# The first block's layers written out, the ends of its layers handed on tile by tile, and the last modulation sum between two tiles

## The chip, the cores and the metric

The kernel runs on one core of a Trainium2 chip. The metric is the device time of one execution in microseconds (us). The engines are PE (TensorE, matrix products), DVE (VectorE), ACT (ScalarE), POOL (GpSimd) and SP (SyncE); SP and POOL issue transfers here. Each engine runs its own instructions in the order in which they are written, and waits for the others on semaphores.

## The reference

x has 256 rows (tokens) of 1024 float32 numbers. A first block of two layers (projections, two kinds of attention, gates, an output projection, a layer norm) is followed by a second block of two layers, whose sublayers are modulated: a shift, a scale and a gate per sublayer come from a conditioning vector c by a product with mod_w.

```python
def first_block(x, w_in, ..., w_out, ln_gamma, ln_beta):
    for l in range(DEPTH):                       # 2
        h = x @ w_in[l]
        ...                                      # MLA and differential attention, gates
        out = merged @ w_out[l]
        x = _layer_norm(DEEPNORM_ALPHA * x + out, ln_gamma[l], ln_beta[l])
    return x

def half_ffn_sublayer(x, mod, j, wi, wo, g, b):
    y = 0.5 * swiglu(modulate(x, mod, j), wi, wo)
    return post_norm_update(x, y, mod, j, g, b)

def second_block(x, c, ctx, c_ctx, mod_w, mod_b, ...):
    for i in range(DEPTH):
        mod_lat = (silu_c @ mod_w[i] + mod_b[i]).reshape(-1, N_MOD, D_MODEL)
        x = half_ffn_sublayer(x, mod_lat, 0, ...)
        mod_ctx = (silu_cc @ mod_w[i] + mod_b[i]).reshape(1, N_MOD, D_MODEL)   # layer 0
        ctx_s = half_ffn_sublayer(ctx_s, mod_ctx, 0, ...)
        ...                                      # window attention (0) or fourier mix (1)
        x = half_ffn_sublayer(x, mod_lat, 2, ...)
```

## The kernel before

The 256 tokens are two tiles of 128 rows, tile 0 and tile 1 (t in the code). Float32 products are made from three matmuls of rounded halves: w_hi by xT_hi, w_lo by xT_hi, w_hi by xT_lo, one after the other (L558, L559, L560), added in one bank (acc0 to acc3). A full projection of 512 columns is 8 such triples for each tile, 48 matmuls for both. The left operand of a product must have its features on the partitions, so x is turned first: PE transposes 128x128 blocks into the banks turn0, turn1, score0 and score1 (L577, or L595 tile by tile), ACT copies them rounded into xT_hi (L1115 plain, L1126 or L1308 with scale and shift of the modulation), and DVE makes xT_lo, the rest (L1490 plain, L1501 and L1502 modulated).

Weights come in pieces of two times 512 columns. SP loads them into raw; ACT rounds one to w_hi (L1087) once PE has freed its place, DVE makes w_lo (L1455). There are 4 places (SPLIT_SLOTS), and the splits run 3 pieces (LEAD) ahead of the projection. A piece is free when tile 1 has used it.

The first block is a loop over LAYERS = 2, in hardware (c.loop) on SP, POOL, PE, ACT and DVE. A wait on a semaphore compares with a register there that grows with the turn of the loop, and REGISTER_ALU instructions compute it; behind the loop the counts are constants. The first projection of a layer is 416 columns wide (LOW). In the loop it is made by project, which takes x turned whole and goes piece by piece, both tiles for each piece. The last projection of a layer, w_out, makes output columns 0 to 511 first (acc0, acc1) and then columns 512 to 1023 by project_by_tile (acc2 for tile 0, acc3 for tile 1): tile 0 with all four pieces, then tile 1 with the same four. first_done is raised behind tile 0.

Behind w_out stands the layer norm. For each tile DVE adds the product to x (L1801), takes the mean (L1544), multiplies (L1549), waits for ACT's square sum and root (L1151, L1153), and writes x (L1555), which raises x_ready. ACT has two splits ahead of its first square sum, and these wait for pieces that tile 1 frees.

Behind some sublayers of the second block (attention, fourier, FFN) the next projection already starts tile by tile: project_first turns tile 0, makes its products with 2 pieces, turns tile 1 and makes the rest. Inside the first block it doesn't.

The modulation vectors of the second block's first layer are made in passing by the first block. POOL loads mod_w chunk by chunk into mod_raw. DVE multiplies a chunk's 8 features by the conditioning and adds them up, for the context and for the latent (L1575, two instructions a feature, the last one into mod_sum_lat); PE sums over the partitions with 4 one-column matmuls for each of the two (mod_sum, L670), and DVE stores the result with the bias (mod_store, L1592, L1593). At a layer's end two chunks are summed: one sum stands between the two halves of w_out's projection, the last one behind it. The features 6 and 7 of the last chunk stand on DVE behind the two additions of acc0 and acc1 and ahead of the norm.

## Time and profile before

| | us |
|---|---|
| median of 3 runs | 1699.57 |
| lowest and highest | 1698.55, 1700.25 |
| the profiled execution, its own time | 1696.36 |
| its span, first to last instruction | 1694.6 |
| PE busy | 1601.3 |
| DVE busy | 1207.7 |
| ACT busy | 802.3 |
| mean granted clock of PE | 0.971 |

The rows further down are from the profiled execution. Their times run from the start of its span. A matmul's length in a row overlaps the next one's start, so that the distance of two starts is what one costs in a row of them. A granted clock of 1.00 is 2.4 GHz, 0.50 is 1.2 GHz.

### The profile page before, as it was taken

What the parts mean: (1) busy time and instruction counts of PE and PEld (TensorE: products, weight loads), DVE (VectorE), ACT (ScalarE), POOL (GpSimd) and SP (SyncE); (2) the same over time, 40 slices, a digit from 0 to 9 for tenths busy, and PEclk for the clock granted to TensorE, in tenths of its full rate; (3) what the DMA queues carried; (4) which work ended last, traced back from release to release, by engine and by line L of the source; (5) the groups of instructions that cost most, each with busy time, mean ns of one, the idle gap of its engine ahead of it and who ended that gap; (6) DMA issues with size and microseconds to landing.
All of it is one profiled execution on the core that took longest, in us unless ns stands there. A gap on an engine that the chain in (4) does not pass through costs nothing.

```text
span 1694.6 us, 23800 instructions
## 1 busy us (share of the span) xinstructions
PE 1601.3 (94%) x7635; PEld 1311.9 (77%) x7635; DVE 1207.7 (71%) x1849; ACT 802.3 (47%) x1242; POOL 140.1 (8%) x205
## 2 busy tenths in 40 slices
PE   6989989989889999999999798999999999989997
PEld 5877778877678878888788457887888878878876
DVE  6877888877887775677757766777487765475545
ACT  5565535455444444444534465444354443254442
POOL 1100001100011110011100011111001110000000
PEclk9999988999989999999999899999999999999999
DMA  8763448743568888588858105988768885466551
GB/s 313 270 208 128 150 152 310 249 169 112 175 219 267 275 270 233 163 280 275 228 181 243 50 1 173 308 275 270 206 212 275 276 232 176 124 177 196 184 183 55
DMA packets 200497, 349.41 MB, mean 206 GB/s; under 512 B 11188, under 2 KB 128236, under 8 KB 199900
## 3 DMA queue, kind: packets, MB, share of 16 engines
q1 hardware_dynamic: 174668, 252.90, 47.2%
q0 software_dynamic: 25744, 95.43, 17.6%
q8 instruction: 47, 0.77, 0.2%
q14 instruction: 38, 0.31, 0.1%
HBM read 347.21 MB, written 1.08 MB: 206 GB/s over the span
## 4 chain that ended last, share of the span: by engine, by line
PE 86%; DVE 8%; issue 3%; ACT 2%; DMA 0%; SPq 0%; DVEq 0%; ACTq 0%
PE acc L558 25%; PE acc L560 25%; PE acc L559 25%; DVE w_lo L1455 2%; PE score L682 2%; PE turn L886 1%; PE acc L794 1%; PE score L973 1%; PE score L670 1%; PE score L774 1%; DVE att_work L2007 1%; PE turn L783 1%; PE score L838 1%; DVE wide L1783 0%; PE score L577 0%
## 5 line engine op out<-in xcount | busy, mean ns | idle before, releaser
L1455 DVE TENSOR_TENSOR w_lo<-raw,w_hi 128x1024 fp32r<-128x1024 f32 (+1 forms) x490 | 586.0, 1200 | 294.3 <-ACT w_hi L1087 287.7
L1087 ACT ACTIVATE w_hi<-raw 128x1024 fp32r<-128x1024 f32 (+1 forms) x490 | 508.2, 1042 | 563.8 <-PE acc L560 561.4
L558 PE MATMUL acc<-w_hi,xT_hi 128*128 128x512 f32 (+1 forms) x1456 | 586.8, 403 | 23.1 <-DVE xT_lo L1502 8.5
L560 PE MATMUL acc<-w_hi,xT_lo 128*128 128x512 f32 (+1 forms) x1456 | 574.6, 395 | 0.0
L559 PE MATMUL acc<-w_lo,xT_hi 128*128 128x512 f32 (+1 forms) x1456 | 574.1, 394 | 0.0
L558 PEld LDWEIGHTS acc<-w_hi,xT_hi 128*128 128x128 f32 x1456 | 279.4, 192 | 83.1 <-issue 25.7
L560 PEld LDWEIGHTS acc<-w_hi,xT_lo 128*128 128x128 f32 x1456 | 278.6, 191 | 59.2
L559 PEld LDWEIGHTS acc<-w_lo,xT_hi 128*128 128x128 f32 x1456 | 279.6, 192 | 54.6
L458 POOL DMA_DIRECT2D mod_raw<-in_mod_w x144 | 104.0, 723 | 963.5 <-DVE mod_run L1575 777.4
L558 PE MATMUL acc<-w_hi,hT_hi 128*128 128x512 f32 x440 | 174.3, 396 | 0.8 <-DVE hT_lo L1916 0.8
L560 PE MATMUL acc<-w_hi,hT_lo 128*128 128x512 f32 x440 | 173.6, 395 | 0.0
L559 PE MATMUL acc<-w_lo,hT_hi 128*128 128x512 f32 x440 | 173.6, 395 | 0.0
L1575 DVE SCALAR_TENSOR_TENSOR mod_run<-mod_raw,silu_c,mod_run 128x512 f32<-128x512 f32 x216 | 161.1, 746 | 4.3 <-DMA mod_raw<-in_mod_w 4.2
L558 PEld LDWEIGHTS acc<-w_hi,hT_hi 128*128 128x128 f32 x440 | 82.8, 188 | 21.1 <-DVE hT_lo L1916 2.0
L560 PEld LDWEIGHTS acc<-w_hi,hT_lo 128*128 128x128 f32 x440 | 82.8, 188 | 19.6
L559 PEld LDWEIGHTS acc<-w_lo,hT_hi 128*128 128x128 f32 x440 | 82.8, 188 | 19.2
L1319 ACT ACTIVATE silu_g<-acc 128x256 f32<-128x256 f32 x110 | 36.2, 381 | 86.8 <-PE acc L560 86.8
L1909 DVE TENSOR_TENSOR hidden<-acc,silu_g 128x256 f32<-128x256 f32 x110 | 41.5, 419 | 16.1 <-ACT silu_g L1319 16.1
L1575 DVE SCALAR_TENSOR_TENSOR acc_ctx<-mod_raw,silu_c,acc_ctx 128x512 f32<-128x512 f32 x70 | 52.2, 746 | 0.0
L1916 DVE TENSOR_TENSOR hT_lo<-turn,hT_hi 128x512 f32 (+1 forms) x55 | 38.0, 692 | 9.7 <-ACT hT_hi L1323 3.5
L1228 ACT ACTIVATE work<-score,neg_max 128x256 f32<-128x256 f32 x64 | 29.7, 473 | 28.8 <-DVE neg_max L1685 28.8
L886 PE MATMUL turn<-ident,hidden 128*128 128x128 f32 x220 | 33.1, 273 | 4.4 <-DVE hidden L1909 4.4
(259 smaller groups left out, 1266.0 us busy)
## 6 DMA issues: line engine op xcount, KB each, us to landing
raw<-in_ffn_wi SPq DMA_DIRECT2D x220, 512.0 KB, 5.0
mod_raw<-in_mod_w POOLq DMA_DIRECT2D x144, 512.0 KB, 4.4
raw<-in_ffn_wo SPq DMA_DIRECT2D x110, 512.0 KB, 4.8
raw<-in_w_in SPq DMA_DIRECT2D x72, 512.0 KB, 5.2
raw<-in_w_out SPq DMA_DIRECT2D x16, 512.0 KB, 4.5
raw<-in_attn_wqkv SPq DMA_DIRECT2D x16, 512.0 KB, 4.6
wide<-in_b_merge POOLq DMA_DIRECT2D x4, 1024.0 KB, 8.3
raw<-in_w_branch_a SPq DMA_DIRECT2D x8, 512.0 KB, 4.2
```

Source lines behind the costliest of these rows:

```text
L458: pool.dma_start(mod_raw[:, s, :, :], w_mod[l, :, 2 * i:2 * i + 2, at]).then_inc(mod_in[s], 16)
L558: nc.tensor.matmul(dst, xh, wh, start=start, stop=False)
L559: nc.tensor.matmul(dst, xh, wl, start=False, stop=False)
L560: return nc.tensor.matmul(dst, xl, wh, start=False, stop=stop)
L682: m = nc.tensor.matmul(bank["score1"][:, 4 * i + j:4 * i + j + 1], mod_kept[:, i, j * P:j * P + P], ones[:, 0:1], start=True, stop=True)
L886: m = nc.tensor.transpose(dst[:, f * TOK + t * P:f * TOK + t * P + P], hidden[:, half, t, f * P:f * P + P], ident[:])
L1087: nc.scalar.activation(w_hi[:, i % SPLIT_SLOTS, 0:n], raw[:, s, i % 2 * PIECE:i % 2 * PIECE + n], ACT.Copy).then_inc(hi_ready, 1)
L1319: nc.scalar.activation(silu_g[:, half, t, :], bank[ACC[2 * half + t]][:, FC:2 * FC], ACT.Silu).then_inc(silu_done, 1)
L1455: nc.vector.tensor_tensor(w_lo[:, i % SPLIT_SLOTS, 0:n], raw[:, i // 2 % RAW_SLOTS, i % 2 * PIECE:i % 2 * PIECE + n], w_hi[:, i % SPLIT_SL ...
L1575: m = nc.vector.scalar_tensor_tensor(out=end if k == KD - 1 else run, in0=w, scalar=by, in1=run, op0=ALU.mult, op1=ALU.add)
L1909: nc.vector.tensor_tensor(hidden[:, half, t, :], bank[b][:, 0:FC], silu_g[:, half, t, :], ALU.mult).then_inc(moved[b], 1)
L1916: nc.vector.tensor_tensor(sl(hT_lo), bank[b][:], sl(hT_hi).bitcast(F32), ALU.subtract).then_inc(moved[b], 1)
```

## The change

1. The loops over the layers of the first block are written out (`for l in range(LAYERS)`) on all five engines, so that counts are constants. piece_width knows the widths of the second layer's pieces too.
2. Each layer's first projection is made by project_first, given the width 416. The norm ahead of it (in ACT's norm_root and DVE's layer_norm) contains the copies of tile 0: plain_tile(0) behind the first layer, turn_tile(0) with the modulation behind the second. Four pieces are split ahead of it, not 3. The start of the kernel, where x comes from memory, has the same order. The second block's first FFN starts by tile too (early=1).
3. PE's last modulation sum of a layer moves from behind project_by_tile to between its tiles. DVE's mod_store of it, with mods_stored, moves from behind the norm to between the addition of acc2 and the mean of tile 0.

```diff
 def piece_width(i):
-    i = i % LAYER_PIECES if i < LAYER_PIECES + LEAD else 0
+    i = i % LAYER_PIECES if i < LAYERS * LAYER_PIECES else 0
...
-            def project_first(banks, kept):
+            def project_first(banks, kept, n=512):
...
-            def project_by_tile(banks):
+            def project_by_tile(banks, between=None):
...
                     if t == 0:
                         m.then_inc(first_done, 1)
+                        if between:
+                            between()
...
-            with c.loop(pe, LAYERS, per):
-                after = turn(lambda t, k: x[:, t, k * P:k * P + P], x_tile)
+            for l in range(LAYERS):
...
-                project(ACC[0:2], 4, n=LOW, after=after)
+                project_first(ACC[0:2], False, LOW)
...
                 project(ACC[0:2], 4, after=after)
                 mod_sum(True)
-                project_by_tile(ACC[2:4])
-                mod_sum(True)
+                project_by_tile(ACC[2:4], lambda: mod_sum(True))
...
-            after = ffn(turn_x(), True, turn_ctx_in, by_tile=False)
+            after = ffn(None, True, turn_ctx_in, by_tile=False)
...
+            def plain_tile(t):
+
+                for half in range(2):
+                    src = filled(turn_bank(2 * t + half))
+                    nc.scalar.activation(xT_hi[:, 4 * half:4 * half + 4, t * P:t * P + P], src[:].rearrange("p (k n) -> p k n", k=4),
+                                         ACT.Copy).then_inc(turn_hi, 1)
+
             split(LEAD)
-            with c.loop(act, LAYERS, per):
-                turn_plain(xT_hi)
+            plain_tile(0)
+            split()
+            for l in range(LAYERS):
+                plain_tile(1)
...
-                norm_root()
+                norm_root(x, SPLIT_SLOTS, (lambda: plain_tile(0)) if l < LAYERS - 1 else (lambda: turn_tile(mod_lat[:, 0, :], 0, 0)))
...
-            nc.scalar.preload_act_table(ACT.Silu)
-            turn_modulated(mod_lat[:, 0, :], 0)
-            ffn(x, True, (mod_ctx, 0))
+            second_tile(0, 0)
+            ffn(x, True, (mod_ctx, 0), early=1)
...
                     add(t, 1)
+                    if t == 0:
+                        mod_store(*ctx_chunk(4))
+                        mods_stored()
...
-                layer_norm(update, lambda t: wide[:, t, 0:D], between=split)
-                mod_store(*ctx_chunk(4))
-                mods_stored()
+                layer_norm(update, lambda t: wide[:, t, 0:D], between=split, at_root=split,
+                           before_end=(lambda: plain_tile(0)) if l < LAYERS - 1 else (lambda: turn_tile(0)))
```

How the instructions stand on the engines, before and after. In these rows the line, the operation, what it writes and reads, its size and the semaphores it waits for are given; the lines of after are those of the changed file.

PE before, the switch from tile 0 (acc2) to tile 1 (acc3) in the last projection of the first layer:

```order
L558 MATMUL acc2<-w_hi,xT_hi 128x512
L559 MATMUL acc2<-w_lo,xT_hi 128x512
L560 MATMUL acc2<-w_hi,xT_lo 128x512
L558 MATMUL acc3<-w_hi,xT_hi 128x512
L559 MATMUL acc3<-w_lo,xT_hi 128x512
L560 MATMUL acc3<-w_hi,xT_lo 128x512
```

PE after, the same place:

```order
L560 MATMUL acc2<-w_hi,xT_lo 128x512
L672 MATMUL score1<-ones,mod_sum_lat 128x1 [waits score1_moved,mod_step]
L672 MATMUL score1<-ones,mod_sum_lat 128x1 x3
L672 MATMUL score1<-ones,acc_ctx 128x1 x4
L558 MATMUL acc3<-w_hi,xT_hi 128x512
L559 MATMUL acc3<-w_lo,xT_hi 128x512
L560 MATMUL acc3<-w_hi,xT_lo 128x512
```

The sum's matmuls (score1) now stand between, with the wait for mod_step, which DVE raises behind each feature.

PE before, behind the last product of that projection, to x's first transposes:

```order
L560 MATMUL acc3<-w_hi,xT_lo 128x512
L666 REGISTER_ALU
L541 REGISTER_ALU [waits mod_step]
L670 MATMUL score1<-ones,mod_sum_lat 128x1 [waits score1_moved]
L670 MATMUL score1<-ones,mod_sum_lat 128x1 x3
L670 MATMUL score1<-ones,acc_ctx 128x1 x4
L112 REGISTER_ALU
L112 COMPARE_AND_BRANCH
L577 MATMUL turn0<-ident,x 128x128 [waits turn0_moved,x_ready]
L577 MATMUL turn0<-ident,x 128x128
L577 MATMUL turn1<-ident,x 128x128 [waits turn1_moved]
```

PE after, the same place:

```order
L560 MATMUL acc3<-w_hi,xT_lo 128x512
L595 MATMUL turn0<-ident,x 128x128 [waits turn0_moved,x_ready]
L595 MATMUL turn0<-ident,x 128x128 x3
L595 MATMUL turn1<-ident,x 128x128 [waits turn1_moved]
L595 MATMUL turn1<-ident,x 128x128 x3
L558 MATMUL acc0<-w_hi,xT_hi 128x416 [waits turn0_moved,lo_ready,acc0_moved]
L559 MATMUL acc0<-w_lo,xT_hi 128x416
L560 MATMUL acc0<-w_hi,xT_lo 128x416
```

The sum and the loop's end are gone; 8 blocks of tile 0 are turned, and its products with 416 columns follow at once.

DVE before, from feature 7 of the last chunk to the next layer:

```order
L1575 SCALAR_TENSOR_TENSOR acc_ctx<-mod_raw,silu_c,acc_ctx 128x512 [waits ctx_step]
L1571 REGISTER_ALU
L1575 SCALAR_TENSOR_TENSOR mod_sum_lat<-mod_raw,silu_c,mod_run 128x512 [waits mod_step]
L1801 SCALAR_TENSOR_TENSOR x,x_sum<-x,acc2 128x512 [waits first_done,ln_in]
L1811 REGISTER_ALU
L1544 SCALAR_TENSOR_TENSOR neg_mean<-x_sum,mean_factor 128x1 [waits acc2_moved]
L1548 REGISTER_ALU
L1549 SCALAR_TENSOR_TENSOR wide<-x,neg_mean,ln_rows 128x1024 [waits mean_ready]
L1554 RECIPROCAL inv_std<-inv_std 128x1 [waits std_ready]
L1461 REGISTER_ALU
L1555 SCALAR_TENSOR_TENSOR x<-wide,inv_std,ln_rows 128x1024 [waits dve_step]
L1453 REGISTER_ALU
```

and behind the norm of tile 1:

```order
L1555 SCALAR_TENSOR_TENSOR x<-wide,inv_std,ln_rows 128x1024 [waits dve_step]
L1464 REGISTER_ALU
L1592 ISA [waits score1_full]
L1592 TENSOR_TENSOR mod_ctx<-score1,modb 128x4
L1593 REGISTER_ALU
L1593 TENSOR_TENSOR mod_lat<-score1,modb 128x4
L1596 MEMSET free 128x1
```

DVE after, the same stretch up to the first copies of the turned tile:

```order
L1598 SCALAR_TENSOR_TENSOR acc_ctx<-mod_raw,silu_c,acc_ctx 128x512 [waits ctx_step]
L1598 SCALAR_TENSOR_TENSOR mod_sum_lat<-mod_raw,silu_c,mod_run 128x512 [waits mod_step]
L1824 SCALAR_TENSOR_TENSOR x,x_sum<-x,acc2 128x512 [waits first_done,ln_in]
L1615 TENSOR_TENSOR mod_ctx<-score1,modb 128x4 [waits score1_full]
L1616 TENSOR_TENSOR mod_lat<-score1,modb 128x4
L1619 MEMSET free 128x1
L1567 SCALAR_TENSOR_TENSOR neg_mean<-x_sum,mean_factor 128x1 [waits acc2_moved]
L1572 SCALAR_TENSOR_TENSOR wide<-x,neg_mean,ln_rows 128x1024 [waits mean_ready]
L1577 RECIPROCAL inv_std<-inv_std 128x1 [waits std_ready]
L1578 SCALAR_TENSOR_TENSOR x<-wide,inv_std,ln_rows 128x1024 [waits dve_step]
L1458 TENSOR_TENSOR w_lo<-raw,w_hi 128x1024 [waits hi_ready]
L1824 SCALAR_TENSOR_TENSOR x,x_sum<-x,acc3 128x512 [waits piece_done]
```

The store of the sum stands between the addition of acc2 and tile 0's neg_mean, and waits there for score1_full.

ACT before, the entry of the loop at the start:

```order
L1087 ACTIVATE w_hi<-raw 128x1024 [waits piece_done,raw_in1]
L112 UNCONDITIONAL_BRANCH
L112 ISA
L1115 ACT_TABLE_LOAD
L1115 ACTIVATE xT_hi<-turn0 128x512 [waits turn0_full]
L1115 ACTIVATE xT_hi<-turn1 128x512 [waits turn1_full]
```

ACT after, the same place:

```order
L1085 ACTIVATE w_hi<-raw 128x1024 [waits piece_done,raw_in0]
L1085 ACTIVATE w_hi<-raw 128x1024 [waits piece_done]
L1085 ACTIVATE w_hi<-raw 128x1024 [waits piece_done,raw_in1]
L1173 ACTIVATE xT_hi<-turn0 128x4x128 [waits turn0_full]
L1173 ACTIVATE xT_hi<-turn1 128x4x128 [waits turn1_full]
```

The loop's entry and its table load are not there.

## Rows read from the trace of the kernel before

**Rows 1.** The page, busy time and share of the engines
```profile
PE 1601.3 (94%) x7635; PEld 1311.9 (77%) x7635; DVE 1207.7 (71%) x1849; ACT 802.3 (47%) x1242; POOL 140.1 (8%) x205
```

**Rows 2.** Timeline of PE, first layer's end: start, us, engine, line, out<-in, idle
```profile
234.67 0.95 PE L670 MATMUL score<-ones,mod_sum_lat 128*128 128x1 f32 x8
236.37 0.48 PE L558 MATMUL acc<-w_hi,xT_hi 128*128 128x512 f32 x1
...
241.94 0.39 PE L558 MATMUL acc<-w_hi,xT_hi 128*128 128x512 f32 x1
```

**Rows 3.** Timeline of DVE, the same stretch
```profile
236.67 0.16 DVE L1592 TENSOR_TENSOR mod_ctx<-score,modb 128x4 f32 x1 [0.89 <-PE score L670]
...
243.89 0.75 DVE L1575 SCALAR_TENSOR_TENSOR mod_sum_lat<-mod_raw,silu_c,mod_run 128x512 f32<-128x512 f32 x1
```

**Rows 4.** Timeline of PE behind tile 1
```profile
247.39 0.95 PE L670 MATMUL score<-ones,mod_sum_lat 128*128 128x1 f32 x8
...
251.02 1.11 PE L577 MATMUL turn<-ident,x 128*128 128x128 f32 x4 [1.79 <-issue]
...
254.20 0.69 PE L577 MATMUL score<-ident,x 128*128 128x128 f32 x2 [1.64 <-DVE mod_lat L1593]
...
257.70 0.71 PE L558 MATMUL acc<-w_hi,xT_hi 128*128 128x416 f32 x1 [1.10 <-DVE xT_lo L1490]
```

**Rows 5.** Timeline of ACT, the same stretch
```profile
254.95 1.28 ACT L1115 ACT_TABLE_LOAD   x1 [2.46 <-issue]
```

**Rows 6.** Windows: us, busy and count of each engine, PEclk, DMA share, GB/s
```profile
257.70:263.40 5.70, 5.70 (x16) 5.44 (x17) 5.70 (x12) 2.61 (x4) 0.00 (x0) 0.50 0.80 277
263.40:269.45 6.05, 6.05 (x33) 6.00 (x32) 6.05 (x8) 2.12 (x2) 0.72 (x1) 1.00 0.80 235
241.94:269.45 27.51, 22.97 (x105) 20.85 (x104) 23.67 (x42) 13.50 (x18) 2.16 (x3) 0.75 0.45 143
478.68:507.80 29.12, 23.39 (x106) 19.40 (x105) 22.49 (x36) 15.21 (x22) 3.25 (x5) 0.82 0.60 209
```

**Rows 7.** Timeline of PE and ACT behind the second block's attention
```profile
1036.91 0.39 PE L560 MATMUL acc<-w_hi,xT_lo 128*128 128x512 f32 x1
...
1039.47 2.91 ACT L1308 ACTIVATE turned_more<-turn,mod_lat 128x128 f32<-128x128 f32 x8 [0.44 <-PE turn L595]
...
1042.59 0.77 PE L558 MATMUL acc<-w_hi,xT_hi 128*128 128x512 f32 x1 [2.79 <-DVE xT_lo L1502]
...
1048.43 1.11 PE L595 MATMUL score<-ident,x 128*128 128x128 f32 x8 [0.38 <-DVE x L1555]
1049.29 0.47 PE L558 MATMUL acc<-w_hi,xT_hi 128*128 128x512 f32 x1
```

**Rows 8.** Timeline of DVE, second layer's end
```profile
480.63 0.75 DVE L1575 SCALAR_TENSOR_TENSOR mod_sum_lat<-mod_raw,silu_c,mod_run 128x512 f32<-128x512 f32 x1
```

**Rows 9.** Timeline of PE and a window, two shorter idle stretches
```profile
169.24 0.49 PE L558 MATMUL acc<-w_hi,xT_hi 128*128 128x512 f32 x1 [1.49 <-DVE wide L1708]
...
457.90 1.93 PE L577 MATMUL score<-ident,wide 128*128 128x128 f32 x8 [3.37 <-DVE wide L1788]
...
461.34 0.44 PE L559 MATMUL acc<-w_lo,xT_hi 128*128 128x512 f32 x1
...
169.20:172.60 3.40, 3.37 (x15) 2.81 (x16) 3.33 (x8) 3.30 (x11) 0.00 (x0) 1.00 0.30 83
```

**Rows 10.** Chain of 30 to 241 by line, one piece; DVE's timeline beside it
```profile
by line: PE acc L558 21.0%; PE acc L560 20.0%; PE acc L559 20.0%; issue 7.0%; PE acc L794 4.6%; DVE w_lo L1455 3.7%; PE score L670 3.2%; PE score L774 3.1%; PE turn L783 2.4%; PE score L838 2.0%; DVE wide L1783 2.0%; DVE acc_ctx L1575 1.2%;
...
201.90 0.50 issue
...
201.74 0.75 DVE L1575 SCALAR_TENSOR_TENSOR acc_ctx<-mod_raw,silu_c,acc_ctx 128x512 f32<-128x512 f32 x1
202.40 0.75 DVE L1575 SCALAR_TENSOR_TENSOR mod_run<-mod_raw,silu_c,mod_run 128x512 f32<-128x512 f32 x1
```

**Rows 11.** Timeline of ACT at the start
```profile
15.69 1.28 ACT L1115 ACT_TABLE_LOAD   x1
```

More of the change, by code:

```diff
@@ L698, in _ @@
             m.then_inc(full[b], 1)
[L700 to L703 removed]
+            for l in range(LAYERS):
                 def turn_latents():
@@ L1493, in turn_plain, with plain_tile @@
                         split_after(g)
+            def plain_tile(t):
+                for half in range(2):
+                    b = turn_bank(2 * t + half)
+                    c.next(b)
+                    dve.wait_ge(turn_hi, c.next("hi"))
+                    sl = lambda r: r[:, 4 * half:4 * half + 4, t * P:t * P + P]
+                    nc.vector.tensor_tensor(sl(xT_lo), bank[b][:].rearrange("p (k n) -> p k n", k=4), sl(xT_hi).bitcast(F32),
+                                            ALU.subtract).then_inc(moved[b], 1)
+                    if t == 0 and half == 0:
+                        split()
             def turn_scaled_group(g, hi, lo, place):
@@ L1605, in _ @@
             split()
-            per = {"split": 64, "piece": 64, "step": 50, "mod": 48, "mod_ctx": 40, "mod_in0": 12, "mod_in1": 12, "turn0": 16, "turn1": 16, "score0": 11, "score1": 17, "acc0": 6, "acc1": 6,
-                   "hi": 10, "low_sq": 1, "low_std": 1, "acc1 moved": 14, "acc3 moved": 12, "bias": 32, "gates": 1,
-                   "diff_sq": DHEADS, "diff_std": 1, "mean": NT, "std": NT, "scaled": 4, "acc2 moved": 12, "ln": 32, "first": 1, "rotated": 1}
-            with c.loop(dve, LAYERS, per) as l:
-                turn_plain(xT_hi, xT_lo, splits=True)
+            plain_tile(0)
+            split()
+            for l in range(LAYERS):
+                split()
+                plain_tile(1)
                 for i, src in enumerate((cols[:, bass.ds(2 * l + G_Q, 1)], cols[:, bass.ds(2 * l + G_Q + 1, 1)],
```

56 lines of the change are left out of this document (25 added, 31 removed).

## The prediction, made before the changed kernel ran

> **What bounds the kernel now.** I read the page's totals first: PE is busy 94% of 1694.6 us [rows 1], the next engine 71%. So the time moves only where PE stands still, runs at the lower of its two clocks, or gets work. The list of PE's idle stretches then says where the change can matter: the end of each layer of the first block. There I read PE's timeline, then DVE's and ACT's beside it, then the windows.
>
> First layer's end. Tile 0 of w_out's projection is over and tile 1 starts at 241.94 [rows 2]. PE ends tile 1, makes the last modulation sum at 247.39, turns x in two bursts with idle of 1.79 and 1.64 us, and starts the next layer's products at 257.70 [rows 4]. The second burst is released by DVE's mod_lat, which stands right behind x of tile 1. ACT loads its table at 254.95, with the turned x waiting [rows 5]. The first 16 products (128x416) then take 5.70 us at a granted clock of 0.50 (1.2 GHz), the 33 behind them 6.05 us at 1.00 (2.4 GHz) [rows 6]. The projection behind that starts at 269.45. From 241.94 that is 27.51 us; the second layer's end, from 478.68 to the FFN's second projection at 507.75, takes 29.1 [rows 6].
>
> The same hand-over by tile as the change makes already runs behind the attention of the second block. Last product 1036.91, so the next slot would be 1037.14; ACT scales the turned tile 0 from 1039.47; products again at 1042.59, 12 of them; tile 1 is turned at 1048.43; products again at 1049.29 [rows 7]. That is 5.45 us to the restart and 5.84 us more to tile 1's turn.
>
> **The change, part by part.**
>
> *1. The last modulation sum between tile 0 and tile 1.* Its 16 one-column matmuls cost 1.70 us (234.67 to 236.37) wherever they stand [rows 2]. But they read what DVE makes of features 6 and 7, and DVE starts the last of these at 243.89 and ends it at 244.64 [rows 3], while PE is through with tile 0 at 241.94. Today that costs nothing, as tile 1 is between. Now PE waits 2.70 us. Queued behind the wait are tile 1's 24 products and all after them. Can DVE come sooner? It waits for the layer's first sum (idle 0.89, released by PE's score at 236.67 [rows 3]) and is busy without a break from there to 244.64: 7.9 us of work against 24 products of PE, 5.57 us. Both are tied to the same instant and the change puts nothing else in between, so the wait is 2.7, with 0.3 of doubt. The second layer's last feature starts at 480.63 and ends at 481.38 [rows 8], tile 0 at 478.68: 2.70 again.
>
> *2. What that wait does to the clock.* No row shows an idle of 2.7 us in a full-speed stretch. The nearest from below: 1.49 us ahead of 169.24, and the window that starts with it stays at 1.00 [rows 9]: nothing lost. From above: 3.37 us ahead of 457.90, after which PE is at half clock until the shorter product of 461.34 [rows 9], 3.4 us of which half is lost, 1.7; the cold stretch of 257.70 to 263.40 would make it 2.85. Idle with 1.7 us of one-column matmuls behind it makes 4.4 us in which PE streams almost nothing, so I lean to the upper row and take 2.0, with 0 to 2.9 as bounds. The Trainium skill, TensorE: Matmul & The Clock Gate, section HAM oscillation, says that a wait between bursts which is long enough makes the next burst start at the low clock, every time over; by it the end would pay twice, here and at the hand-over; it also means that a shorter one is free, and then the sum would be 2.0 less at each end.
>
> *3. Hand-over by tile, first end.* PE ends tile 1 at 241.94 + 2.70 + 1.70 + 5.45 + 2.0 = 253.8 (5.45: window of 241.94 to 247.39, the rows' difference). The restart comes 5.45 later in the row behind the attention. Here ACT makes 2 plain copies for its 8 scaled ones of 2.91 us [rows 7], and DVE drops the cast and the gate's multiply. DVE's other work between stays, so not all of that is won; I estimate 1.0 less, so 4.4: 258.2. Tile 1 is turned 5.8 later, 264.0, as DVE and ACT do the same norm between. The 12 narrow products ahead of it hide in that. Turning takes 0.86 at full clock (1048.43 to 1049.29), 1.7 at half; 1.3, since 4.2 us of cold products with idle behind are less than the 5.70 that it took today. The 36 products left take 36 x 0.19 = 6.8, plus 0.5 for those still cold. Next projection: 264.0 + 1.3 + 6.8 + 0.5 = 272.6, against 269.45: **+3.1**.
>
> Without the wait and its cold stretch (4.7) it would be 267.9, 1.6 better than now: the hand-over by tile is worth that, and the moved sum costs more.
>
> *4. Second end.* The same to 478.68 + 11.85 = 490.5. Restart 5.2 later (scaled copies stay; only the gate's multiply is gone), 495.7; to the products of tile 1's second part 6.7 as behind the attention; then 36 products of 128x512 at 0.2275, 8.2: 510.6 against 507.75: **+2.8**.
>
> *5. The start.* The table load of 1.28 us at the loop's entry [rows 11] is not there in the changed order, and PE waits for what stands behind it. Given back: tile 1 is now turned between products (0.9 to 1.7), where it was hidden before. -0.4 to +0.4 by that alone; tile 1's products also need a fourth piece split earlier, on DVE, and PE can start after half the work: -1.3 at best, +0.5 at worst, I take **-0.5**.
>
> *6. The loops written out.* Register arithmetic, the jump back and the ACT table load at the loop's head go. The jump's 1.79 us of PE idle (released by "issue", 251.02 [rows 4]) ended before x of tile 1 was there, so it hid behind DVE. I take 0; from 0 to what the third rival says. Register work ahead of DVE's instructions leaves no gap: at 201.74 two follow one another 0.66 apart, with no idle listed between [rows 10]. DVE's store of the sum now stands ahead of tile 0's norm and waits for PE until 246.4. Behind the store are neg_mean and one product of x, done by about 248.5; what x of tile 0 then waits for is ACT's root, which stands behind two splits that need the first two pieces freed by tile 1 (246.3 + 2.9, a split and the squares: past 251). So the store is hidden by over 2 us; without that cover each us of it would be a us. Loads on SP's and POOL's queues keep their order; transfers are not what PE waits for here.
>
> Sum: 3.1 + 2.8 - 0.5 = **+5.4 us**. The profiled run took 1696.36 with a span of 1694.6; it would be 1701.8 now. The median of the runs shown is 1699.57, 3.2 above the profiled run, so I forecast 1699.57 + 5.4 = **1705.0**. A measurement of this kernel can tell about 0.2%, 3.4 us, from no change.
>
> **Rivals.**
>
> *A. The forecast*, wait and cold stretch at both ends: 1703 to 1707.
>
> *B. The wait is there but the clock holds*, as behind the 1.49 us idle. Each end 2.0 better, +1.4 in all, 1701.0; with half of it lost, +3.4. For it: 2.7 is nearer to 1.49 than to 3.37. Against it: the matmuls of one column behind it. It gives "the same". The rule of the Trainium skill named above has room for both.
>
> *C. The other side: the loops cost more than their gaps show.* The chain of waits of 30 to 241 gives "issue" 7.0%, 14.8 us of a layer, 29.6 in two [rows 10]; pieces of it are 0.50 us long inside DVE's work. Were that register arithmetic, writing out would take a third of it away: -10, with the +5.4 of the rest the time is 1695.0. It decides from 5.4 us, a fifth of this share; under it the kernel isn't faster. Against it: DVE's rows lie end to end there, so the "issue" is time of an instruction that overlaps its neighbour's.
>
> *D. It gets worse.* If PE is at half clock also for the 12 products, tile 1's turn and the whole of the rest, because the two gaps leave too little between them, each end loses 2 more (the 36 narrow products at 0.35 for 12 of them): +9.4, 1709.
>
> **How the numbers follow.** A 0.52, B 0.26, C 0.12, D 0.10. B lies inside 0.2%, C is faster, A and D slower: 0.12, 0.26, 0.62. The range takes all of A and B (down to +0.5 for a gain of 1.3 at the start, 1700.1), most of D, up to 1709.0, and the near part of C, down to 1697.5, where writing out would be worth 7.5.
>
> **What will show it.** Right: in each layer's end an idle of 2.7 us ahead of the sum's first matmul, released by DVE's mod_sum_lat; 24 products of tile 1 of which the first ones stand 0.427 apart; the restart 4.4 (5.2) behind the last; tile 1's turn 5.8 later; no table load at the start. The stretch from tile 0's end to the next projection is 30.6 and 31.9 us. B: products 0.2275 apart right behind the sum. C: the middle of each layer, from 30 to 230, is shorter by more than 2 us with the same PE work. Wrong altogether would be an end with no idle at the sum, since all rests on DVE being as late as it is now.

## The result, and the profile after

The changed kernel takes 1716.91 us (median of 4 runs, 1716.32 to 1719.07); the kernel before took 1699.06 beside it. The ratio is 1.0112, with a 95% interval of 1.0097 to 1.0127: about 18 us slower, where 5.4 were forecast. The forecast had the sign and missed the range, which ended at 1709.0. The profiled execution has a span of 1715.2 us, 20.6 more than before; the medians are 17.9 apart, since the profiled execution of before (1696.36) was 2.7 us under its median and this one (1716.99) lies on it.

To find where they come from, one takes the same piece of work in both traces and subtracts its starts. The stages are cut at products that can be told by their shape: the first product of 512 columns of a layer (its second projection), the first of 384 columns, the switch from tile 0 to tile 1 in w_out.

| Stretch | before | after | longer by | forecast |
|---|---|---|---|---|
| span's start to the first layer's second projection | 30.34 | 29.02 | -1.3 | -0.5 |
| first layer: second projection to the 384-column products | 60.2 | 67.5 | +7.3 | 0 |
| from there to the switch of tiles | 151.4 | 149.4 | -2.0 | 0 |
| first end: switch to the next layer's second projection | 27.5 | 30.5 | +3.0 | +3.1 |
| second layer: second projection to the 384-column products | 60.2 | 66.8 | +6.6 | 0 |
| from there to the switch of tiles | 149.0 | 149.9 | +0.8 | 0 |
| second end: switch to the FFN's second projection | 29.1 | 33.3 | +4.2 | +2.8 |
| everything behind it | | | +2.0 | 0 |
| sum | | | +20.6 | +5.4 |

So the three places that the forecast looked at came out within 1.4 us of it, and two thirds of the loss lie where it said nothing: at the beginning of each layer, some 20 us behind the hand-over.

The page of the changed kernel, busy time and the chain by engine. Against [rows 1], PE has 6 us more of busy time for the same 7635 instructions (products at half clock), DVE's work is the same, and 2% of the chain that ended last is now DMA, where it was 0%:

```profile
PE 1607.4 (94%) x7635; PEld 1314.3 (77%) x7635; DVE 1206.8 (70%) x1849; ACT 801.6 (47%) x1248; POOL 140.5 (8%) x205
...
PE 81%; DVE 13%; ACT 3%; DMA 2%; issue 2%; SPq 0%; DVEq 0%; ACTq 0%
```

**The beginning of a layer.** PE's timeline behind the first layer's second projection (start, us, engine, line, out<-in, count, and in brackets the idle time ahead and who ended it):

```profile
49.88 0.50 PE L558 MATMUL acc<-w_hi,xT_hi 128*128 128x512 f32 x1 [1.61 <-DVE w_lo L1458]
...
57.57 0.76 PE L558 MATMUL acc<-w_hi,xT_hi 128*128 128x512 f32 x1 [2.95 <-DVE w_lo L1458]
```

PE waits for a split of weights twice, 1.61 and 2.95 us, and is at half clock behind the second wait: eleven products from 57.57 on, 0.63 us long instead of 0.39 and 0.43 apart instead of 0.23, which is some 2.3 us more. The three together are 6.9 of the 7.3 us. Neither wait is there before. DVE's timeline says what it did instead of splitting:

```profile
26.98 1.23 DVE L1458 TENSOR_TENSOR w_lo<-raw,w_hi 128x1024 fp32r<-128x1024 f32 x1 [2.83 <-ACT w_hi L1085]
28.12 0.48 DVE L1596 TENSOR_SCALAR acc_ctx<-mod_raw,silu_c 128x512 f32<-128x512 f32 x1
...
48.60 1.22 DVE L1458 TENSOR_TENSOR w_lo<-raw,w_hi 128x1024 fp32r<-128x1024 f32 x1
55.41 0.49 DVE L1596 TENSOR_SCALAR acc_ctx<-mod_raw,silu_c 128x512 f32<-128x512 f32 x1 [5.58 <-DMA mod_raw<-in_mod_w]
...
56.20 1.22 DVE L1458 TENSOR_TENSOR w_lo<-raw,w_hi 128x1024 fp32r<-128x1024 f32 x1
```

Read the brackets. At 26.98 DVE waited for ACT's w_hi of the fifth piece. The first two features stand behind that split, so they come at 28.12; before, at 23.66, though PE's products started 1.5 us later then. Then at 55.41 DVE waits 5.58 us for a DMA: the second chunk of mod_w. The split at 56.20 is queued behind it, and that is the one that PE wants at 57.57.

Why was the fifth piece late? ACT, the same time:

```profile
16.44 1.05 ACT L1085 ACTIVATE w_hi<-raw 128x1024 fp32r<-128x1024 f32 x1
21.99 1.09 ACT L1173 ACTIVATE xT_hi<-score 128x512 fp32r<-128x512 f32 x2 [4.50 <-PE score L595]
25.89 3.32 ACT L1085 ACTIVATE w_hi<-raw 128x1024 fp32r<-128x1024 f32 x3 [2.81 <-PE acc L560]
```

ACT waits 2.81 us for a product of PE to free a place. A piece is free when tile 1 has used it. In the projection piece by piece that is after 12 products; tile by tile it is after 30, with the turning of tile 1 among them: 24 of tile 0 and 6 of tile 1.

Why was the chunk late? POOL's timeline of the changed kernel, from the third load of the first chunk to the first load of the second chunk:

```profile
31.76 0.72 POOL L458 DMA_DIRECT2D mod_raw<-in_mod_w  x1 [21.36 <-DVE mod_run L1598]
36.68 0.72 POOL L458 DMA_DIRECT2D mod_raw<-in_mod_w  x1 [4.20 <-DVE mod_run L1598]
37.40 1.11 POOL L485 DMA_DIRECT2D wide<-in_b_merge  x2
38.50 0.53 POOL L466 DMA_DIRECT2D ln_rows<-in_ln_gamma  x1
39.02 0.53 POOL L467 DMA_DIRECT2D ln_rows<-in_ln_beta  x1
41.60 0.72 POOL L458 DMA_DIRECT2D mod_raw<-in_mod_w  x1 [2.04 <-DVE mod_run L1598]
```

and of the kernel before:

```profile
27.64 0.72 POOL L458 DMA_DIRECT2D mod_raw<-in_mod_w  x1 [16.49 <-DVE mod_run L1575]
...
33.49 1.11 POOL L485 DMA_DIRECT2D wide<-in_b_merge  x2
...
38.11 0.72 POOL L458 DMA_DIRECT2D mod_raw<-in_mod_w  x1 [2.47 <-DVE mod_run L1575]
```

POOL issues in order, and its third load waits for DVE's first two features: 31.76 against 27.64. Behind it in the queue stand another mod load, the merge bias (2 x 1 MB) and the norm's rows (2 x 0.5 MB), and only then the second chunk: 41.60 against 38.11. That is 3.5 us later; but the load landed 13.8 us after its issue (55.4), where before it took 11.6 (49.7). Windows of the changed kernel (us, busy and count of PE, PEld, DVE, ACT, POOL, then PEclk, DMA share, GB/s):

```profile
26.00:34.00 8.00, 8.00 (x39) 7.11 (x39) 7.02 (x10) 6.01 (x7) 0.72 (x1) 1.00 0.33 105
42.00:56.00 14.00, 11.01 (x56) 8.98 (x54) 7.24 (x23) 8.06 (x17) 1.05 (x2) 0.99 1.02 399
```

From 26 to 34 the transfers run at a third of their time with nothing to fetch, and from 42 to 56 the transfers come at 399 GB/s, with the 3 MB among them. (Before, they are as dense from 40 to 50 us, at 398 GB/s, but the chunk's load was issued earlier.) The chunk lands 5.7 us later than before: 3.5 by its issue and 2.2 by its longer way.

**The ends of the layers.** PE at the first end, from tile 0's last product to the second projection's neighbour; it answers to [rows 2] and [rows 4]:

```profile
245.69 0.39 PE L560 MATMUL acc<-w_hi,xT_lo 128*128 128x512 f32 x1
248.45 1.05 PE L672 MATMUL score<-ones,mod_sum_lat 128*128 128x1 f32 x8 [2.37 <-DVE mod_sum_lat L1598]
...
250.34 0.77 PE L558 MATMUL acc<-w_hi,xT_hi 128*128 128x512 f32 x1
...
258.97 1.10 PE L595 MATMUL turn<-ident,x 128*128 128x128 f32 x8 [1.41 <-DVE x L1578]
...
261.66 0.68 PE L558 MATMUL acc<-w_hi,xT_hi 128*128 128x416 f32 x1 [1.59 <-DVE xT_lo L1505]
...
268.64 0.70 PE L558 MATMUL acc<-w_hi,xT_hi 128*128 128x416 f32 x1
```

The idle ahead of the sum is there and released by DVE's mod_sum_lat: 2.37 us (2.7 were forecast from where PE's next product would start; counted so, 245.91 to 248.45, it is 2.54). The products start at half clock (0.77), the restart is 4.3 behind tile 1's last slot (forecast 4.4), tile 1's products another 7.0 on. The second end:

```profile
495.65 1.64 PE L672 MATMUL score<-ones,mod_sum_lat 128*128 128x1 f32 x8 [2.38 <-DVE mod_sum_lat L1598]
497.15 1.84 PE L672 MATMUL score<-ones,acc_ctx 128*128 128x1 f32 x8
498.86 0.77 PE L558 MATMUL acc<-w_hi,xT_hi 128*128 128x512 f32 x1
...
511.40 0.77 PE L558 MATMUL acc<-w_hi,xT_hi 128*128 128x512 f32 x1 [2.50 <-DVE xT_lo L1517]
```

Here the sum itself ran at half clock, 1.64 and 1.84 us where it takes 0.95 and 1.03 [rows 4], 3.2 from start to start instead of 1.7. That is 1.5 us which the forecast did not have, and it missed 1.4 at this end. From its first product to the slot behind its last, tile 1 takes 7.1 us at the first end (250.34 to 257.40) and 7.4 at the second, for 5.45 of work. Windows of it, each to the end of its last product, granted clock 0.78 and 0.74:

```profile
250.34:257.56 7.22, 7.22 (x25) 5.52 (x25) 1.78 (x6) 3.71 (x6) 0.00 (x0) 0.78 0.00 0
498.86:506.42 7.56, 7.56 (x25) 5.74 (x25) 1.81 (x6) 3.73 (x6) 0.00 (x0) 0.74 0.00 0
```

### The profile page after: what moved, and what is told of

It reads as the page before. It is cut to its first block, busy times and chain, and to the rows that moved or that the text cites. A ratio compares the mean times of both kernels' runs of the same rounds, so it can differ in the third digit from the quotient of the medians.

```text
span 1715.2 us, 22567 instructions
## 1 busy us (share of the span) xinstructions
PE 1607.4 (94%) x7635; PEld 1314.3 (77%) x7635; DVE 1206.8 (70%) x1849; ACT 801.6 (47%) x1248; POOL 140.5 (8%) x205
## 4 chain that ended last, share of the span: by engine, by line
PE 81%; DVE 13%; ACT 3%; DMA 2%; issue 2%; SPq 0%; DVEq 0%; ACTq 0%
PE acc L558 24%; PE acc L560 23%; PE acc L559 23%; DVE w_lo L1458 4%; DMA mod_raw<-in_mod_w 2%; PE score L684 1%; PE turn L884 1%; PE acc L793 1%; DVE x L1578 1%; PE score L672 1%; PE score L971 1%; DVE acc_ctx L1598 1%; PE score L773 1%; DVE att_work L2024 1%; ACT w_hi L1085 1%
## 5 line engine op out<-in xcount | busy, mean ns | idle before, releaser
L558 PEld LDWEIGHTS acc<-w_hi,xT_hi 128*128 128x128 f32 x1456 | 281.0, 193 | 94.7 <-issue 30.5
```

The source lines that it names most:

```text
L558: nc.tensor.matmul(dst, xh, wh, start=start, stop=False)
```

## The experiments

Times are medians, each beside runs of the kernel before on the same chip; a ratio is to that kernel, with its 95% interval. "Changed kernel" is the one that was predicted. The kernel before took 1699.06 us beside the changed kernel, 1698.55 beside experiments 1 to 4, 1700.12 beside 5 to 7 and 1701.29 beside 8 to 10, so a difference of two medians from different groups is uncertain by 2 to 3 us.

### 1. Only the loops written out

```diff
-            with c.loop(dve, LAYERS, per) as l:
+            for l in range(LAYERS):
```

(the same on the other four engines, in the kernel before)

> The kernel before with only the loops over the layers written out on all five engines (and the widths of the second layer's pieces). Theory 1 (the first projection by tile frees its pieces late, DVE's features of the modulation start late, their loads with them, and DVE then stands in front of its splits): no effect here, 1698 to 1700 us, no wait of DVE for mod_raw over 1.1 us. Theory 2 (written-out code delays the loads or the engines' issue): 1705 us or more, with PE idle near 48 and 54 us as in the changed kernel. The forecast's rival C (register arithmetic is dear) would give under 1695.

Measured: 1695.48 us, ratio 0.9984 (0.9970 to 0.9997). Written-out code does not make the stall: in its trace PE stands nowhere between 30 and 88 us for over 1.2 us. It is a little faster than the kernel before. PE at its first product (18.43 before) and behind the first chunk's sum:

```profile
17.19 0.43 PE L558 MATMUL acc<-w_hi,xT_hi 128*128 128x416 f32 x1 [2.71 <-DVE xT_lo L1490]
...
51.95 0.47 PE L558 MATMUL acc<-w_hi,xT_hi 128*128 128x512 f32 x1 [0.47 <-DVE w_lo L1455]
...
52.84 0.63 PE L558 MATMUL acc<-w_hi,xT_hi 128*128 128x512 f32 x1
```

The first product comes 1.2 us earlier; the table load that the loop's entry needed [rows 11] is not there. DVE's wait for the second chunk is 3.2 us here, where it was 0.6 before, and it has a price: PE waits 0.47 us for the split behind it, and its next products are at half clock (0.63) until 55.83. The stretch from the second projection to the 384-column products is 62.4 us, 2.2 more than before. So a late load can cost something even with the features in time, but not the stall of the changed kernel.

The expectation missed twice: DVE's wait was to stay under 1.1 us, and the time at 1698 to 1700. The rival of over 1705 is out, and so is the one of under 1695, by little.

Writing out also shortens the first layer's end: from the switch of tiles (239.60) to the next second projection (264.98) it takes 25.4 us, 2.1 less than before. ACT's table load of 254.95 [rows 5] is gone from there, the products restart 15.0 us behind the switch instead of 15.8, and they are at half clock for 2.9 us (granted clock 0.52 from 254.59 to 257.50) and not for 5.7 [rows 6].

### 2. The sum behind tile 1 again

```diff
-                project_by_tile(ACC[2:4], lambda: mod_sum(True))
+                project_by_tile(ACC[2:4])
+                mod_sum(True)
...
-                    if t == 0:
+                    if t == 1:
                         mod_store(*ctx_chunk(4))
```

> The changed kernel with the last modulation sum behind tile 1 again; DVE stores it behind the addition of tile 1. From the changed kernel's trace the stretch from tile 0's end to tile 1's last product is 11.5 and 13.2 us where 5.45 is the work: 6.0 and 7.7 are the wait, the sum and the half clock. Theory 1 expects 1716.9 - 13.7 + 0.6 (the sum no longer quite hidden) = 1704 us, with the stalls near 48 and 54 us unchanged. If the ends cost what they cost because of the hand-over by tile and not of the sum, it is over 1711.

Measured: 1701.97 us, ratio 1.0017 (1.0003 to 1.0032), 15 us less than the changed kernel; about 1704 was expected. PE at the first end:

```profile
251.31 0.95 PE L672 MATMUL score<-ones,mod_sum_lat 128*128 128x1 f32 x8
...
253.02 1.07 PE L595 MATMUL turn<-ident,x 128*128 128x128 f32 x8
...
255.59 0.42 PE L558 MATMUL acc<-w_hi,xT_hi 128*128 128x416 f32 x1 [1.50 <-DVE xT_lo L1506]
...
260.96 1.97 PE L595 MATMUL score<-ident,x 128*128 128x128 f32 x8 [2.86 <-DVE x L1579]
262.58 0.69 PE L558 MATMUL acc<-w_hi,xT_hi 128*128 128x416 f32 x1
```

No wait ahead of the sum, the turn right behind it, a restart after 1.50 us of idle, and the products 0.42 and then 0.35 long: there the clock held. It fell at the second idle, of 2.86 us: the turn of eight blocks behind it took 1.97 us instead of 1.07, and the first products of tile 1 0.69 and 0.55. The stretch from the switch to the next second projection is 24.1 us, 3.4 less than in the kernel before and 6.4 less than in the changed one. The 6.4 are the moved sum. The 3.4 are not all the hand-over by tile: writing out alone gives 2.1 of them (experiment 1), so the hand-over gives 1.3. At the second end it is 26.7 us, against 29.1 before and 28.9 written out. The stalls of 1.28 and 3.10 us at 48 and 54, and of 1.61 and 2.98 in the second layer, are unchanged, as expected: they have nothing to do with the sum. They need the first projection by tile (part 2 of the change): experiments 1 and 4, which are written out but make it piece by piece, don't have them. Which item of part 2 makes them, the order of the products or the four pieces split ahead, no run separates.

### 3. Two features ahead of the first split

```diff
-                split_and_mod(7, range(8), True)
+                mod_feature(0, True)
+                mod_feature(1, True)
+                split_and_mod(7, range(2, 8), True)
```

> The changed kernel with features 0 and 1 of each layer's first chunk put on DVE ahead of the first split instead of behind it, where DVE stands idle for 2.8 and 3.8 us. Theory 1: feature 0 starts 4 us earlier, POOL's third load too, the wait of 5.6 and 5.8 us for mod_raw falls under 2, PE's idle of 1.6 and 2.9 us near 48 and 54 goes: 11 to 14 us less, 1703 to 1706. Rival (the loads are late because of what stands in their queue, not because of when DVE frees the buffer): wait and stalls stay, 1713 or more.

Measured: 1703.57 us, ratio 1.0034 (1.0020 to 1.0048), 13 us less than the changed kernel and inside the expectation. DVE of this kernel:

```profile
24.19 0.48 DVE L1596 TENSOR_SCALAR acc_ctx<-mod_raw,silu_c 128x512 f32<-128x512 f32 x1
...
27.11 2.36 DVE L1458 TENSOR_TENSOR w_lo<-raw,w_hi 128x1024 fp32r<-128x1024 f32 x2 [0.72 <-ACT w_hi L1085]
...
50.94 0.49 DVE L1596 TENSOR_SCALAR acc_ctx<-mod_raw,silu_c 128x512 f32<-128x512 f32 x1 [3.00 <-DMA mod_raw<-in_mod_w]
```

Feature 0 starts at 24.19 instead of 28.12, in the time in which DVE stood idle; the wait ahead of the next split shrinks to 0.72; the wait for the second chunk is 3.00 instead of 5.58, where under 2 was expected. PE has no idle over 1.2 us from 17 to 88 us, and the 384-column products of the two layers start at 89.79 and 330.18, against 96.55 and 343.26. So with the features in time the late load costs PE next to nothing here: its longest wait for a split in that stretch is 0.31 us, at 53.10. One order of instructions, with no work more or less, is 13 us.

### 4. Only the sum moved, in the kernel before

The kernel of experiment 1 with the two edits of part 3 of the change (PE's `between`, DVE's store in `update(0)`).

> The kernel before, loops written out, with only the move of the last modulation sum between the tiles (and of its store); first projections as before. Parts 1 and 2 of the forecast alone, with the sizes of the changed kernel's trace: 2.4 us wait, the sum of 1.7 to 3.2, half clock behind it, 6.0 + 7.7 = 13.7 less what the sum behind tile 1 costs today (hidden behind the wait for x, 0 to 1): 1711 to 1713 us. Rival: the move is cheap where x isn't handed on by tile, under 1706.

Measured: 1707.99 us, ratio 1.0057 (1.0040 to 1.0075): 12.5 more than experiment 1, where the expectation was 1711 to 1713. PE at the first end:

```profile
242.54 1.05 PE L672 MATMUL score<-ones,mod_sum_lat 128*128 128x1 f32 x8 [2.38 <-DVE mod_sum_lat L1576]
...
244.34 0.69 PE L558 MATMUL acc<-w_hi,xT_hi 128*128 128x512 f32 x1
```

The same wait, the same fall of the clock. That is 6 us for each end, whether x is handed on by tile or not. It started from a kernel 3 us faster than the expectation had put it, which is its miss.

### 5. The 3 MB ahead, with the features late

```diff
-                mod_load(0, bass.ds(l * (5 * 512), 512))
+                mod_load(0, bass.ds(l * (5 * 512), 512), range(2))
                 for t in range(NT):
                     pool.dma_start(wide[:, t, GATES:GATES + 2 * D], ...)
                 norm_rows(a["ln_gamma"][l], a["ln_beta"][l])
+                mod_load(0, bass.ds(l * (5 * 512), 512), range(2, 4))
```

> The changed kernel with POOL's loads of the merge bias (2 x 1 MB) and of the norm's rows (2 x 0.5 MB) issued right behind the layer's first two mod loads, ahead of the third and fourth, which wait for DVE's features. Theory 1 says that DVE's lateness holds these 3 MB back until they stand in front of the second chunk's load (13.8 us to land against 4.4 to 7 elsewhere). Then here the second chunk's first load lands within 7 us, DVE's wait of 5.6 and 5.8 us falls under 1.5, PE's idle near 49 and 54 us of the span goes, and the time falls by 8 to 13 us, to 1704 to 1709; at the start of the kernel the 3 MB compete with the first weights, which may cost up to 4. If DVE's start alone is what counts and not the transfers ahead, the wait stays over 4 us.

Measured: 1714.45 us, ratio 1.0091 (1.0074 to 1.0108), where 1704 to 1709 was expected: a miss. (The profiled execution took 1710.22, with a span of 1708.5.) DVE's waits for mod_raw from 12 to 120 us (us in total, times, longest), and PE:

```profile
DVE acc_ctx L1599 <- DMA mod_raw<-in_mod_w: 1.6, 1, 1.6
...
50.39 0.50 PE L559 MATMUL acc<-w_hi,xT_hi 128*128 128x512 f32 x1 [2.21 <-DVE w_lo L1459]
```

The wait for the second chunk is gone, so the 3 MB did make it. The second stall, near 54, is gone too. But PE still stands 2.21 us ahead of 50.39, for a split. DVE is as late with its features as in the changed kernel, and now it also waits 1.6 us at 39.02 for a load of the first chunk, which was issued behind the 3 MB. From the second projection to the 384-column products it takes 64.3 and 64.6 us in the two layers, against 67.5 and 66.8 of the changed kernel and 60.2 before. The median fell by only 2.5.

### 6 and 7. Both repairs, and the 3 MB ahead too

Experiments 2 and 3 together; then with the edit of 5 on top.

> The changed kernel with both repairs: the last sum behind tile 1, and features 0 and 1 ahead of the layer's first split. Each alone gave about 15 and 13 us; they act at different places, so together 1716.9 - 15 - 13 = 1689, 1687 to 1691 us, under the kernel before (1698.6). If the two share a cause (PE late, so that transfers meet otherwise) the sum falls short: 1695 or more.

Measured: 1692.50 us, ratio 0.9961 (0.9948 to 0.9974): faster than the kernel before. It falls short of the expected 1687 to 1691. DVE and PE of its second layer say why:

```profile
285.99 0.49 DVE L1597 TENSOR_SCALAR acc_ctx<-mod_raw,silu_c 128x512 f32<-128x512 f32 x1 [4.96 <-DMA mod_raw<-in_mod_w]
...
288.15 0.77 PE L558 MATMUL acc<-w_hi,xT_hi 128*128 128x512 f32 x1 [2.27 <-DVE w_lo L1459]
```

The second chunk again arrives 5 us late, in the second layer alone, and PE waits 2.27 us for the split behind it. The first layer's end is shorter here, and the second layer's loads are issued when its x is done; that this is why they meet more traffic is my reading, and no run shows it.

This kernel has the end of experiment 2, instruction by instruction. PE's restart there:

```profile
248.73 0.69 PE L558 MATMUL acc<-w_hi,xT_hi 128*128 128x416 f32 x1 [1.50 <-DVE xT_lo L1506]
```

The idle ahead of it is the same 1.50 us and it is released by the same instruction, but the product takes 0.69 us and not 0.42: half clock. So it is in experiments 7 and 10 (0.69), and in experiment 9 it is 0.43.

> As the one ahead of it, and POOL's bias and norm rows early too. DVE's wait for the second chunk is 3 us there with features first and lies in DVE's slack, so theory 1 expects nothing more: 1687 to 1692 us; up to 3 more if the early 3 MB delay the first weights.

Measured: 1697.29 us (twelve runs, from 1693.3 to 1701.8), ratio 0.9989 (0.9975 to 1.0003), 5 more than without. Expected was no change. In its trace (an execution of 1700.07 us) DVE waits 6.9 us for mod_raw in the second layer and PE stands 4.3 us at 279.46. There the 3 MB go out at x's end, together with the layer's first mod chunk and weights. Loads that nobody waits for soon do not get cheaper by going first.

### 8 to 10. The 3 MB behind the second chunk

```diff
-                for t in range(NT):
-                    pool.dma_start(wide[:, t, GATES:GATES + 2 * D], ...)
-                norm_rows(a["ln_gamma"][l], a["ln_beta"][l])
                 mod_load(0, bass.ds(l * (5 * 512) + 512, 512))
+                for t in range(NT):
+                    pool.dma_start(wide[:, t, GATES:GATES + 2 * D], ...)
+                norm_rows(a["ln_gamma"][l], a["ln_beta"][l])
```

in the changed kernel, in the kernel of experiment 2, and in that of experiment 6.

> The changed kernel with the loads of the merge bias and the norm's rows (3 MB a layer) issued behind the second chunk's mod loads instead of ahead of them; nothing waits for them before the gates. DVE's features are as late as in the changed kernel. If the saturated transfers (12 to 14 us at about 400 GB/s with these 3 MB among them) make the second chunk's first load land after 13.8 us, it lands within 8 us here, DVE's waits of 5.6 and 5.8 us fall under 2. The time falls by 4 to 8 us, to 1709 to 1713: PE's stall at the layer's first part becomes shorter, but DVE stays 4 us late with its splits, as with the loads early (whose span was 6.7 us shorter). If DVE's lateness alone makes the stall, nothing changes: 1716.

Measured: 1708.25 us, ratio 1.0047 (1.0030 to 1.0063), 8.7 less than the changed kernel. PE has no idle over 1.2 us between 17 and 89 us. DVE and POOL of this kernel:

```profile
75.22 0.49 DVE L1596 TENSOR_SCALAR mod_run<-mod_raw,silu_c 128x512 f32<-128x512 f32 x1 [6.89 <-DMA mod_raw<-in_mod_w]
...
58.24 1.10 POOL L486 DMA_DIRECT2D wide<-in_b_merge  x2
...
62.44 0.72 POOL L458 DMA_DIRECT2D mod_raw<-in_mod_w  x1 [2.04 <-DVE mod_run L1598]
```

The wait for the second chunk is gone, as expected, and a new one has come: DVE waits 6.89 us for the third chunk, whose load at 62.44 stands behind the 3 MB. But at 75 us DVE is ahead of PE, and nobody notices. A wait as long as the one that cost PE's stall costs nothing 20 us later.

I had expected PE's stall to become shorter only, since DVE's features are as late as before (POOL's third load at 31.85). It went nearly whole: PE's longest wait for a split there is 0.75 us, at 49.10, and the clock holds behind it. From the second projection to the 384-column products it takes 61.3 us in both layers, against 67.5 and 66.8 in the changed kernel, 60.6 and 60.4 in experiment 3 and 60.2 before. So lateness alone costs 1.1 us a layer. It takes both, the late features and the 3 MB in front of the second chunk, to make the stalls, and taking away either one gives nearly all of it back.

> Sum behind tile 1 and the 3 MB late, features in the changed kernel's place. From the run with the sum behind (1702.0) less 4 to 8: 1694 to 1698 us.

Measured: 1693.53 us, ratio 0.9956 (0.9940 to 0.9971), half a us under the expected 1694 to 1698.

> Sum behind tile 1, features 0 and 1 ahead of the first split, and the 3 MB late. In the run without the last of these (1692.5) DVE still waited 5.0 us for the second chunk in the second layer and PE stood 2.3 us. That goes: 1687 to 1690 us, the fastest of all. If the second layer's stall has another cause (weights that land late), 1692.

Measured: 1690.96 us, ratio 0.9944 (0.9931 to 0.9958), the fastest: 0.6% under the kernel before and 26 us under the changed one. The expectation said 1687 to 1690, so it is a little short. (By the two ratios to the kernel before, 0.9944 and 1.0112, it is 29 us under the changed kernel.) DVE's waits in its second layer from 255 to 330 us, with PE never idle there for over 1.2 us until 323:

```profile
DVE mod_run L1597 <- DMA mod_raw<-in_mod_w: 6.6, 1, 6.6
DVE acc_ctx L1597 <- DMA mod_raw<-in_mod_w: 1.7, 1, 1.7
```

One wait of 6.6 us and one of 1.7 that cost nothing, since they lie where DVE has time; the stretch to the 384-column products is 60.4 us in both layers. PE's 2.27 us of experiment 6 are gone, so it was the second chunk's load and not the weights.

## Why the prediction was wrong

**Part 1, the moved sum: right.** Idle 2.37 us in both ends, released by the feature that was named. Experiment 4 is that part alone, experiment 2 all but it.

**Part 2, the clock: right in kind.** 2.0 us were put down for the half clock behind the wait; tile 1 took 7.1 and 7.4 us for 5.45 of work, 1.6 and 1.9. Rival B is out: behind 2.4 us of idle and the sum PE was at half clock at both ends, and in experiment 4 too. By the Trainium skill's rule (TensorE: Matmul & The Clock Gate, section HAM oscillation) a wait that is long enough is paid again each time by the burst behind it. These two ends agree: 1.6 and 1.9 us at the first burst, and the restart behind it is cold again (0.68 at 261.66, 0.77 at 511.40). Missed was that the sum's own matmuls can be inside the cold stretch (3.2 us for 1.7 at the second end).

The prediction tried to place 2.7 us between an idle of 1.49 that left the clock alone and one of 3.37 that did not. The runs show that the length of the idle does not decide by itself. Behind 1.50 us in the same place PE was at full clock in two traces (experiments 2 and 9) and at half in three (6, 7 and 10). And the longer idle, the turn ahead of w_out behind 3.37 us (3.64 when written out), was followed by half clock in every trace but that of experiment 5, where it was full in both layers (1.09 us for eight blocks, not 1.97):

```profile
221.07 1.09 PE L578 MATMUL score<-ident,wide 128*128 128x128 f32 x8 [3.64 <-DVE wide L1812]
```

It also takes no idle at all: from 686.43 of the kernel before, PE makes the 48 one-column matmuls of another sum (score from ones and mod_kept, L682) without a break, 6.9 us behind products at full clock, and the next product takes 0.77 us and its neighbours 0.63. This fits the prediction's argument, which counted the sum's one-column matmuls with the idle. That its 2.0 came so near to 1.6 and 1.9 is in part luck, since either of the two rows that it stood between could have gone the other way.

**Parts 3 and 4, the hand-over by tile: right in length, and the terms fit** (4.3 for 4.4, 5.14 for 5.2, 6.7 for 6.7). The side remark that without the sum the first end would be 1.6 us shorter was too low: it is 3.2 to 4.3 in experiments 2, 6, 7, 9 and 10 (24.3 to 23.2 us for 27.5). 2.1 of that is writing out, which part 6 put at nothing; 1.1 to 2.2 are left to the hand-over by tile.

**Part 5, the start: -1.3 for -0.5**, its best end, and by luck. Written out alone, the second projection starts at 27.86 and 28.73 (experiments 1 and 4), against 29.02 in the changed kernel and 28.3 to 29.3 in the others by tile. So the gain is the loop's, and the order by tile gave nothing there.

**Part 6: wrong, and with it the sum.** It says that loads on POOL's queue "keep their order; transfers are not what PE waits for here". The order was kept; the times were not. The step that failed is this one, a term put at nothing, and it rests on one before: in parts 3 and 5 I priced project_first by PE's rows alone, as a stretch of work that ends at the layer's second projection. What I never asked is who waits for the pieces that it gives back. By tile, the first piece comes back when tile 1 has used it, after 30 products and not after 12. ACT's fifth split waits for it (2.81 us), DVE's fifth split for ACT (2.83), the features for DVE, POOL's third load for the features (4.1 later), 3 MB and the second chunk for POOL; DVE waits 5.6 us for that chunk with a split behind it, and PE waits for the split. Every link was in the order of the changed kernel: `split` ahead of the features, seven splits instead of eight. The row behind the attention [rows 7], from which I took the hand-over's price, could not warn me: there no features and no queue stand behind the freed pieces. What it cost: 7.3 and 6.6 us, 13.9 of the 15.2 that the sum was short. The two causes do not add up, they need each other: experiment 3 takes away the lateness, experiment 8 the 3 MB in front, and each gives back nearly all (60.6 and 61.3 us for 67.5). Experiment 5 has the 3 MB out of the second chunk's way but in that of the first, and gives back less than half (64.3).

Part 6 also put the written-out loops at nothing at the layer's end, since the jump's idle hid behind DVE. The jump's did, but ACT's table load did not, and the half clock behind it was longer: 2.1 us at the first end (experiment 1). Against the written-out kernel, whose first end takes 25.4 us, the changed kernel loses 5.1 us there and not 3.0.

**Rival C, dear loops: wrong in size, not in sign.** Writing out alone is worth 3.1 us (ratio 0.9984), not 10. By stretches its trace has -2.5 us at the start, +2.2 to the 384-column products (DVE's wait for the second chunk and the half clock behind it), -2.1 to the switch, -2.1 at the first end, 0 and +2.3 in the second layer, -0.2 and +0.2 behind it. The -2.1 to the switch (-2.0 in the changed kernel) is no gain of the loops: in these twelve traces the middle of a layer, from the 384-column products to the switch, takes from 146.9 to 151.9 us, and in experiment 1 it is shorter in the first layer and longer in the second by the same amount. The 7.0% of "issue" in the chain was no price for it, as the argument against the rival said.

**What stays open.** The 2.0 us behind the second end. 1.6 of them arise at one place, the sum of the kept modulations and the products behind it (686.43 to 697.06 in the kernel before, from 705.02 on in the changed one): the same instructions, more of them at half clock. They are not the change's. In these traces what is behind the second end takes 1186.7 to 1187.1 us where that sum took 6.6 to 7.3 (the kernel before, experiments 1, 2, 4 and 6), and 1188.4 to 1189.2 where it took 7.7 to 8.1 (the changed kernel and experiments 3, 5 and 7 to 10). Kernels with and without each part of the change stand on both sides. What decides the side no run shows; I have none that moves the moment by a known amount. Also open is what sets the level behind the idle of 1.50 us and behind that of 3.64.

## What to carry to other kernels

When a product is made tile by tile, its weights come back later, though it ends no later: follow the freed buffer through the engines and queues behind it, and ask at each link what else is in that queue. Put work that frees a transfer's buffer ahead of a step that may wait, if it can stand there; two features ahead of one split were 13 us of 1717. A stall can need two causes at once, and then either repair is enough. And a wait has no price of its own: 5.6 us of DVE's waiting went with a loss of 7.3 us at 55 us, 3.2 of it with 2.2 us in experiment 1, and 6.9 of it with none at 75. When two parts are changed together, run each alone before giving one of them a price: 2.1 of the 3.4 us that the first end gains in experiment 2 are the written-out loops', and not the hand-over's.

## What the runs showed of the hardware

The transfers of one core reached about 400 GB/s in the crowded stretch (399 from 42 to 56 us, DMA share 1.02), and a 512 KB load issued into it landed after 13.8 us, where the median of these loads is 4.6. Eight of the sum's one-column matmuls took 0.95 us at full clock [rows 4], 1.05 behind 2.37 us of idle at the first end, and 1.64 behind the same idle at the second: the same work at either level, by its moment. The product behind 1.50 us of idle took 0.42 us and its neighbours 0.35 in experiment 2, full clock, and 0.69 and 0.55 in experiment 6, half clock, in the same place of the same instructions. In experiment 1 the clock fell behind a sum of one-column matmuls and an idle of only 0.47 us, and behind 48 one-column matmuls in a row it was at its half in each of the twelve traces, with no idle ahead of the next product.
